# Opening of a two-block transformer kernel: small bias-table copies, two tiles in three sweeps, x split ahead of the weights

## The reference, cut to what matters

```python
h = rmsnorm(x, g[0])                       # x: 256 x 2048
z = h @ w_in                               # 2048 x 6016, in 47 tiles of 128 output channels
# attention of the first block, over head h and query/key distance
bucket = t5_causal_bucket(np.clip(delta, 0, steps) * dilation)
bias = jnp.transpose(rel_bias_table.astype(jnp.float32)[bucket], (2, 0, 1))
# second block
lam = (jnp.exp(jnp.sum(lam_q1[l] * lam_k1[l])) - jnp.exp(jnp.sum(lam_q2[l] * lam_k2[l])) + lam_init)
```

## Time and profile before

| | us |
|---|---|
| median of 3 runs | 3179.52 (3177.28 to 3184.86) |
| span of the profiled execution | 3175.2 |
| time of the profiled execution beside its span | not given; median less span is 4.3 |
| PE busy | 3039.0 (96%) |
| DVE busy | 1571.8 (50%) |
| ACT busy | 1267.2 (40%) |
| DMA, mean rate | 160 GB/s |

### The profile page before, as it was taken

The page is one execution under the profiler, slowest core; times in us unless marked ns, Lnnn a source line. Parts: engine busy times, 40 slices in busy tenths (PEclk is TensorE's granted clock), DMA queues, the critical chain, the costliest instruction groups (busy, mean ns, idle before and its releaser), DMA issues.

```text
span 3175.2 us, 52130 instructions
## 1 busy us (share of the span) xinstructions
PE 3039.0 (96%) x21592; PEld 2647.1 (83%) x21592; DVE 1571.8 (50%) x2406; ACT 1267.2 (40%) x1929; POOL 17.9 (1%) x34
## 2 busy tenths in 40 slices
PE   6999999899889999999998999999999999999997
PEld 6966666698779999999996888778878998889896
DVE  4444444544365556564445323554553474247754
ACT  3322112343445444443334223444442472245544
POOL 0000000000000000000000000000000000000000
PEclk9999999999989999999999999999999999999998
DMA  7568777544435555545553222222223443234342
GB/s 230 185 268 316 318 311 307 199 141 150 146 119 183 179 181 185 181 156 182 174 191 112 93 93 80 80 80 90 85 100 125 159 160 106 88 121 146 136 156 107
DMA packets 74280, 509.71 MB, mean 161 GB/s; under 512 B 8460, under 2 KB 8588, under 8 KB 20240
## 3 DMA queue, kind: packets, MB, share of 16 engines
q1 hardware_dynamic: 70416, 486.08, 42.9%
q0 software_dynamic: 3712, 21.40, 2.1%
HBM read 500.89 MB, written 6.55 MB: 160 GB/s over the span
## 4 chain that ended last, share of the span: by engine, by line
PE 87%; DVE 6%; ACT 3%; DMA 3%; issue 1%; SPq 0%; ACTq 0%; DVEq 0%
PE bank L685 40%; PE bank L1240 8%; PE bank L800 5%; PE bank L1271 5%; PE bank L1273 5%; PE bank L1272 5%; DMA high_f<-in_w_in 2%; PE bank L817 2%; PE bank L730 1%; PE bank L731 1%; PE bank L732 1%; PE bank L896 1%; PE bank L956 1%; DVE ring_f32r L1996 1%; PE bank L1309 1%
## 5 line engine op out<-in xcount | busy, mean ns | idle before, releaser
L1996 DVE TENSOR_TENSOR ring_f32r<-ring_f,high_f32r 128x1024 fp32r<-128x1024 f32 (+1 forms) x692 | 781.1, 1160 | 795.3 <-ACT high_f32r L1425 794.1
L1425 ACT CAST high_f32r<-ring_f 128x1024 fp32r<-128x1024 f32 (+1 forms) x692 | 655.8, 997 | 881.9 <-PE bank L685 536.2
L685 PE MATMUL bank<-y_f32r,high_f32r 128*128 128x256 f32 (+1 forms) x2784 | 853.1, 306 | 23.6 <-DVE ring_f32r L1996 11.2
L685 PE MATMUL bank<-h_f32r,high_f32r 128*128 128x256 f32 (+1 forms) x2208 | 685.8, 311 | 3.4 <-DVE y_f32r L1996 3.4
L685 PE MATMUL bank<-y_f32r,ring_f32r 128*128 128x256 f32 (+1 forms) x2208 | 673.9, 305 | 0.0
L685 PEld LDWEIGHTS bank<-y_f32r,high_f32r 128*128 128x128 f32 x2784 | 535.9, 192 | 47.4 <-issue 22.5
L685 PEld LDWEIGHTS bank<-h_f32r,high_f32r 128*128 128x128 f32 x2208 | 422.9, 192 | 25.3 <-issue 4.5
L685 PEld LDWEIGHTS bank<-y_f32r,ring_f32r 128*128 128x128 f32 x2208 | 424.9, 192 | 17.2
L1271 PE MATMUL bank<-h_f32r,high_f32r 128*128 128x512 f32 x512 | 209.3, 409 | 0.0
L800 PE MATMUL bank<-h_f,high_f 128*128 128x256 f32 x768 | 195.8, 393 | 11.1 <-DMA high_f<-in_w_in 10.9
L1273 PE MATMUL bank<-h_f32r,ring_f32r 128*128 128x512 f32 x512 | 200.1, 391 | 0.0
(11 more groups left out here) (415 smaller groups left out, 4960.1 us busy)
## 6 DMA issues: line engine op xcount, KB each, us to landing
ring_f<-in_w_in SPq DMA_DIRECT2D x135, 1024.0 KB, 4.9
ring_f<-in_w_mod SPq DMA_DIRECT2D x96, 1024.0 KB, 9.1
ring_f<-in_w_up SPq DMA_DIRECT2D x88, 1024.0 KB, 4.9
ring_f<-in_w_out SPq DMA_DIRECT2D x56, 1024.0 KB, 4.9
ring_f<-in_w_down SPq DMA_DIRECT2D x64, 704.0 KB, 4.1
high_f<-in_w_in SPq DMA_DIRECT2D x24, 1024.0 KB, 5.0
ring_f<-in_w_kv SPq DMA_DIRECT2D x8, 1024.0 KB, 5.0
ring_f<-in_w_q SPq DMA_DIRECT2D x4, 1024.0 KB, 4.8
```

Of the source, the lines that this page charges most:

```text
L685: last = mm(bk[(t0 + j) % banks][:, 0:width], w[:, c], x[:, k], start=(k == 0 and w is hi and x is rhs.hi), stop=(k == KC - 1 and w is lo))
L1425: act.copy(w_hi[p % 2][:, half], slot[s % SLOTS][:, half]).then_inc(w_high, 1)
L1996: return v.tensor_tensor(out, in0, in1, op)
```

## The change

There are five edits.

1. `skew` holds 8 copies of each line where it held 128 (`SHIFTS`), so the write moves 96 rows of 1.5 KB and not 1536. Reading it back takes 16 loads of 8 partitions, each from another starting point, and DVE waits for all 16.
2. POOL's loads of constants wait for slab 1 to have landed, where they waited for the last quarter of x.
3. ACT rounds slab 1 before it rounds the input.
4. DVE makes all four quarters of the input, then takes their rests, then `low` of slab 0 and of slab 1.
5. PE runs tiles 0 and 1 together in three sweeps (`first_two`): high x high of both, high x rest of both, rest x high of both, and only then the matmuls of the bias lines and of `lam`.

```diff
+SHIFTS = 8
 # gpsimd
-            pool.wait_ge(S("x_loaded3"), 16)
+            pool.wait_ge(w_in_slot[1], 16)
             load(kmix, d["k_mix"], "mix_loaded")
...
             pool.wait_ge(S("lam_line_made"), 2)
-            pool.dma_start(d["skew"].rearrange("(h p n) -> h p n", p=P, n=384),
-                           g_line[0:A_HEADS, :].rearrange("h (a n) -> h a n", a=1).to_broadcast([A_HEADS, P, 384])
+            pool.dma_start(d["skew"].rearrange("(h p n) -> h p n", p=SHIFTS, n=384),
+                           g_line[0:A_HEADS, :].rearrange("h (a n) -> h a n", a=1).to_broadcast([A_HEADS, SHIFTS, 384])
                            ).then_inc(S("line_stored"), 16)
...
-            skewed = d["skew"].rearrange("(h x) -> h x", h=A_HEADS)[:, 127:127 + 383 * P]
             pool.wait_ge(S("rw_kksq"), C_TILES)
-            load(G, skewed.rearrange("h (p n) -> p h n", n=383)[:, :, 0:T], "G_loaded")
+            for g in range(P // SHIFTS):
+                lines = bass.AP(d["skew"].tensor, P - 1 - SHIFTS * g, [[383, SHIFTS], [SHIFTS * 384, A_HEADS], [1, T]])
+                load(G[SHIFTS * g:SHIFTS * (g + 1)], lines, "G_loaded")
 # tensor
-                tile(0, 0, opening_waits)
+                tile(0, 0, opening_waits and name != "in1")
...
+            def first_two():
+                r = RHS["in1"]
+                for part in range(3):
+                    for j in range(2):
+                        if part == 0:
+                            pe.wait_ge(w_high, 2 * j + 2)
+                        elif part == 2:
+                            pe.wait_ge(w_split, j + 1)
+                        w, x = (w_lo if part == 2 else w_hi)[j], (r.lo if part == 1 else r.hi)
+                        for k in range(KC):
+                            if j == 0 and part < 2 and k % 4 == 0:
+                                pe.wait_ge(rhs_split if part else rhs_high, RHS0["in1"] + k // 4 + 1)
+                            last = mm(bk[j][:, 0:T], w[:, k * P:(k + 1) * P], x[:, k],
+                                      start=(part == 0 and k == 0), stop=(part == 2 and k == KC - 1))
+                        if part == 2:
+                            last.then_inc(gemm_done, 1)
+            first_two()
             pe.wait_ge(loaded, 16)
             pe.wait_ge(S("mix_loaded"), 16)
             mm(bk[2][0:A_HEADS, 0:384], vec("table")[0:33, :], kmix[0:33, 0:384], start=True, stop=True
...
-            gemm3("in1", 0, 23)
+            gemm3("in1", 2, 21)
 # scalar
             high("in1", 0)
+            high("in1", 1)
             rhs_highs("in1")
-            high("in1", 1)
 # vector
+            make = norm_quarter(H[0], X[0], gains(0))
+            for q in range(4):
+                make(q).then_inc(rhs_made, 1)
+            for q in range(4):
+                rhs_low("in1", q)
             low("in1", 0)
-            rhs_made_and_split("in1", norm_quarter(H[0], X[0], gains(0)))
             low("in1", 1)
...
-            dve.wait_ge(S("G_loaded"), 16)
+            dve.wait_ge(S("G_loaded"), 16 * P // SHIFTS)
 # build
-    d["skew"] = nc.dram_tensor("skew", (A_HEADS * P * 384,), F32, kind="Internal").ap()
+    d["skew"] = nc.dram_tensor("skew", (A_HEADS * SHIFTS * 384,), F32, kind="Internal").ap()
```

## The result

The changed kernel takes 3187.0 us (median of 20 runs, 3182.2 to 3190.5), the kernel before 3178.9 beside it: a ratio of 1.0025, with a 95% interval from 1.0019 to 1.0031, so 8 us slower. 3174.9 was forecast, within 3170.5 and 3179.0. The opening came out as forecast: tile 5 is counted 0.2 us from the forecast time. The loss is in turn six, 500 us later, where the forecast put 0: it is the mechanism of rival 4, which had 4 in 100.

A forecast was written before the change was run, and what follows sets the result against it. PE was taken to bound the kernel, with an 11.1 us stall behind skew's write. Tile 5 at 42.55 + 4 x 5.76 + 0.3 + 1.9 = 67.8 against 72.44, G's load 0: 3179.5 - 4.6 = 3174.9, range 3170.5 to 3179.0.

The forecast's parts named there:

- rival 4: Turn six: 16 small loads choke the slabs, one landing after 21.8 us, up to 13.4 us PE idle; 3188.3, chance 0.04.
- The load of G: Turn six: one load becomes 16 with the same bytes, a slab's 8.4 against 6.3 us stays; taken as 0.
- The write of skew: Opening: the write shrinks to a sixteenth, 2.2 us by proportion, at most 8.7; the stall of 11.1 us goes.
- The start: Opening: first sweep starts at 20.45, sweeps end at 36.3 against tile 1's 38.3; gain 2.0 us.
- What is queued behind it: Opening: ACT's and DVE's work for tile 2 waits behind bias lines and lam; tile 2 starts at 42.6, not 38.1.
- The clock: Opening: after 5.1 us of idle PE, tile 2 starts at the low clock; loss 1.5 to 2.6 us, 1.9 taken.
- Sum of the opening: Tile 5 counted at 67.8 against 72.44, a gain of 4.6 us.
- Rivals 1, 2 and 3: Opening: clock holds or chain shorter, 3172.5 (0.21); all the stall comes back, 3166.4 (0.06); start later, 3177.6 (0.11).

The follow-up runs named there:

- e8: e7 with the matmuls of the bias lines and lam ahead of the three sweeps, and k_mix loaded ahead of slab 1's landing: 3166.7 us (0.9965).
- e7: The changed kernel with its 8 copies spread to 128 by a second memory-to-memory write and G read by one load: 3174.2 us (0.9984).
- e15: The changed kernel with the bias-line and lam matmuls ahead of the sweeps and the small loads of G issued late: 3167.4 us (0.9956).
- e6: The changed kernel with its 16 small loads issued in another order, alternating between the partition halves: 3184.0 us (one run).
- e1_skew_only: The kernel before with edit 1 alone (8 copies, 16 small loads): 3182.4 us (1.0011).

## Why the prediction was wrong

The step that failed is "The load of G": "The bytes are the same, so beside it a slab's 8.4 against 6.3 stays. I take 0". The bytes are the same, but not the rate at which they can be put away. The term put at 0 measured 11.6 us in the trace and 12.8 by the runs (12.1 in the pair without edits 2 to 5). The step took one of the two ways in which a load can delay a slab, its bytes, and left out the other, how long its packets hold the engines: 97.7% of their time for 0.57 MB in the worst 6 us.

- **The write of skew.** Right: 11.1 us of stall gone, the write landing in 5.1. The signs were there for the step that failed: 2304 KB in 35.4 us are 65 GB/s, out of 12 partitions, and this step read them as a matter of bytes and rows alone. Rival 4 did read them so.
- **The start.** Right to 0.7: first sweep 20.71 for 20.45, the sweeps' end 37.0 for 36.3, of which 0.4 is x that landed later in this execution.
- **What is queued behind it.** Right, and the best-founded step: PE's idle 5.15 us for 5.1, tile 2 at 43.28 for 42.55. `e8` shows the cause by undoing it.
- **The clock.** Right here: 3.3 us at half clock, a loss of 1.4 for the 1.9 taken. It is not a fixed term: 5.16 idle us in `e7`, as good as the same, were followed by 5.8 us at half clock. `e8` and `e15` have the pair with and without.
- **Sum of the opening.** Tile 5 counted at 68.0 for 67.8. That it is 0.2 is partly luck: tile 2 starts 0.7 late, and the clock gives 0.5 back.
- **Rivals 1, 2 and 3** failed with the forecast. **Rival 4** was right in mechanism. Its time, 3188.3 for the measured 3187.0, is partly luck: it had the slab landing after 21.8 us and PE idle by 13.4 more, and measured are 15.9 and 7.5; the low clock behind the wait, two later waits and 2.2 us of clock elsewhere, none of them in its sum, made up the rest. Its chance of 0.04 was the mistake. Two arguments stood against it: that each number of `G` goes to another place and that the loads are issued one by one. Both are true of the changed kernel and of `e6`, and neither helped.
- The tell-tale given in advance, a slab near 516 to 525 us that takes over 10, is what the profile shows.
- **The rest of the difference**, 8.9 - 6.7 = 2.2 us behind `G`'s first reader, is not of the change's making. 1.3 of it: PE idles 2.70 us at 1422 in the changed kernel as it does at 1415 in the other (2.69), but here the clock falls, and there it doesn't. 0.9 more: in the last 21 us of the program both run at half clock, and the changed kernel for longer. The wait at 1422:

```profile
1422.51 0.58 PE L1257 MATMUL bank<-y_f32r,high_f32r 128*128 128x256 f32 x1 [2.70 <-DVE ring_f32r L2013]
```

The stretch behind it:

```profile
1422.60:1425.50 2.90, 2.90 (x14) 2.90 (x15) 1.46 (x2) 0.00 (x0) 0.00 (x0) 0.50 0.22 91
```

Before, the 4 us behind the idle have the full clock:

```profile
1416.00:1420.00 4.00, 4.00 (x36) 4.00 (x35) 1.07 (x2) 0.22 (x1) 0.00 (x0) 1.00 0.08 34
```

This wait is in all 17 profiled runs, 2.69 to 2.71 us long, with the full clock and the same work ahead of it. The clock has fallen behind it in nine of them and not in eight.

## What to carry to other kernels

A transfer cut by partitions is another transfer, even if no byte is added: loads that fill few neighbouring partitions brought the whole core's DMA rate down to about a quarter here in their worst 6 us (108 GB/s for 385), because their packets hold the engines that the other queue's transfers need. Weigh it by what PE is waiting for at that moment, and prefer cuts that leave each piece all 128 partitions. And when work is put first in a program, follow each wait of the work that is left behind it: two matmuls of 1 us cost 6 to 7.5 us here, 4.8 of them because ACT and DVE had the next tile queued behind them, the rest by the clock. Where the forecast has a rival whose price is three times the gain, and a row of the same kind already runs slow, its chance is not 4 in 100.

## What the runs showed of the hardware

- With one load to 128 partitions on its way beside slabs, the core moves 385 to 397 GB/s; with small loads to 8 neighbours 108 beside slabs and 131 alone, at a DMA share of over 1 each time: the busy share doesn't tell how much the engines move.
- A packet of 4 KB took 0.17 us to a load that fills 128 partitions, 0.24 and 0.25 to 32 neighbours and to 16 that lie 8 apart, 0.33 to 0.48 to 16 or 8 neighbours.
- Memory to memory, 2304 KB landed in 9.1 to 11.7 us (six runs); out of 12 partitions in 35.4.
- The same idle stretch of PE left the clock up with 2.69 us (`before`) and 2.71 (`e1_skew_only`, `e15_first_and_late`), and was followed by half clock with 2.69 (`e8_lines_first`) and 2.70 (the changed kernel); so the length alone doesn't decide it.
